# Latent attention scores: the rotary matmul over 128 partitions with half of them zero, in place of 64 partitions

## The reference, cut to what matters

```python
q = rms_norm(q, g_q); k = rms_norm(k, g_k)            # per head, 192 = 128 + 64 columns
q = concat([q[..., :128], rope(q[..., 128:], pos)])    # 64 rotary columns
k = concat([k[..., :128], rope(k[..., 128:], pos)])    # rotary key is shared by all heads before the norm
s = einsum('bqhe,bkhe->bhqk', qb, k) * 192 ** -0.5     # causal, then softmax, then @ v
```

## Time and profile before

| | |
|---|---|
| median of 3 runs | 1491.66 us (1490.26 to 1491.86) |
| span of the profiled execution | 1489.8 us |
| PE busy | 1456.9 us (98%) |
| PE weight loads busy | 1260.5 us (85%) |
| DVE, ACT, POOL busy | 43%, 46%, 48% |
| latent stage with its attention | about 76 to 342 us of the span |
| dilated stage | about 420 to 1400 us |

### The profile page before, as it was taken

One profiled execution on the slowest core, in us unless ns is written; L12 is line 12 of the kernel. 1 busy time (PEld: TensorE's weight loads), 2 busy tenths in 40 slices (PEclk: granted clock), 3 DMA queues, 4 the chain that ended last, 5 costly groups with the idle time before them and its releaser, 6 DMA issues.

```text
span 1489.8 us, 22557 instructions
## 1 busy us (share of the span) xinstructions
PE 1456.9 (98%) x8018; PEld 1260.5 (85%) x8018; DVE 635.0 (43%) x1024; ACT 686.8 (46%) x975; POOL 708.4 (48%) x332
## 2 busy tenths in 40 slices
PE   6999999999999999999999999999999999999998
PEld 4888888899988888888888888888887888888998
DVE  7455566544953234333334333433342333333332
ACT  4354555544334445444544544444544544444442
POOL 3443444433545444644553554564465355445432
PEclk9899999999999999999999999999999999999999
DMA  6443334335545554654554554555455455455444
GB/s 235 156 148 131 130 123 141 134 128 184 169 167 187 190 175 145 191 190 150 180 191 157 170 189 151 170 187 179 147 187 190 151 179 191 150 177 192 162 156 142
DMA packets 69344, 248.50 MB, mean 167 GB/s; under 512 B 7696, under 2 KB 8080, under 8 KB 69136
## 3 DMA queue, kind: packets, MB, share of 16 engines
q1 hardware_dynamic: 69120, 246.28, 48.7%
q10 hardware_dynamic: 144, 1.05, 0.2%
HBM read 245.20 MB, written 2.10 MB: 166 GB/s over the span
## 4 chain that ended last, share of the span: by engine, by line
PE 38%; issue 31%; POOL 26%; DVE 4%; POOLq 0%; DMA 0%; ACT 0%; SPq 0%; ACTq 0%; DVEq 0%
PE acc L1069 35%; POOL w_lo L378 21%; POOL root L392 2%; DVE xa_lo L712 1%; POOL phase L438 1%; POOL rms L389 1%; PE turn L1099 1%; PE pv_bank L1111 1%; PE score L1289 1%; DVE w_lo L698 1%; DVE prob L743 0%; DVE xb_hi L709 0%; POOL rms L396 0%; DVE xa_hi L709 0%; DVE res L980 0%
## 5 line engine op out<-in xcount | busy, mean ns | idle before, releaser
L378 POOL TENSOR_TENSOR w_lo<-raw,w_hi 128x1024 fp32r<-128x1024 f32 x232 | 574.1, 2475 | 636.5 <-ACT w_hi L462 636.3
L462 ACT ACTIVATE w_hi<-raw 128x1024 fp32r<-128x1024 f32 (+1 forms) x465 | 485.4, 1050 | 342.8 <-PE acc L1069 331.8
L698 DVE TENSOR_TENSOR w_lo<-raw,w_hi 128x1024 fp32r<-128x1024 f32 (+1 forms) x233 | 313.2, 1345 | 439.7 <-ACT w_hi L462 439.7
L1069 PE MATMUL acc<-w_hi,xa_hi 128*128 128x512 f32 (+1 forms) x1088 | 407.0, 374 | 10.7 <-DVE w_lo L698 10.7
L1069 PE MATMUL acc<-w_hi,xa_lo 128*128 128x512 f32 (+1 forms) x1088 | 399.0, 367 | 0.0
L1069 PE MATMUL acc<-w_lo,xa_hi 128*128 128x512 f32 (+1 forms) x1088 | 398.2, 366 | 0.0
L1069 PE MATMUL acc<-w_hi,xb_hi 128*128 128x512 f32 (+1 forms) x640 | 252.6, 395 | 4.3 <-POOL w_lo L378 2.4
L1069 PE MATMUL acc<-w_hi,xb_lo 128*128 128x512 f32 (+1 forms) x640 | 247.4, 387 | 0.0
L1069 PE MATMUL acc<-w_lo,xb_hi 128*128 128x512 f32 (+1 forms) x640 | 247.3, 386 | 0.0
L1069 PEld LDWEIGHTS acc<-w_hi,xa_hi 128*128 128x128 f32 x1088 | 206.6, 190 | 44.5 <-issue 13.4
L1069 PEld LDWEIGHTS acc<-w_hi,xa_lo 128*128 128x128 f32 x1088 | 206.2, 190 | 33.8
(11 more groups left out here) (116 smaller groups left out, 1076.1 us busy)
## 6 DMA issues: line engine op xcount, KB each, us to landing
raw<-in_w_b SPq DMA_DIRECT2D x320, 512.0 KB, 3.3
raw<-in_w_gate SPq DMA_DIRECT2D x32, 512.0 KB, 3.2
raw<-in_w_out_a SPq DMA_DIRECT2D x32, 512.0 KB, 3.3
raw<-in_w_out_b SPq DMA_DIRECT2D x32, 512.0 KB, 3.3
raw<-in_w_in SPq DMA_DIRECT2D x16, 512.0 KB, 4.3
raw<-in_w_kv SPq DMA_DIRECT2D x16, 512.0 KB, 3.3
raw<-in_w_q SPq DMA_DIRECT2D x16, 384.0 KB, 3.0
res<-in_xT SPq DMA_DIRECT2D x4, 512.0 KB, 7.3
```

The costliest lines, as they stand in the source:

```text
L378: nc.gpsimd.tensor_tensor(w[1][:, s, 0:width], raw[:, s, 0:width], w[0][:, s, 0:width].bitcast(F32), ALU.subtract).then_inc(lo_ready[1], 1)
L462: nc.scalar.activation(w[0][:, s, 0:width], raw[:, s, 0:width], ACT.Copy).then_inc(hi_ready, 1)
L698: nc.vector.tensor_tensor(w[1][:, s, 0:width], raw[:, s, 0:width], w[0][:, s, 0:width].bitcast(F32), ALU.subtract).then_inc(lo_ready[0], 1)
L1069: last = nc.tensor.matmul(out, x(a), y(b), start=start and k == 0, stop=stop and k == 2, **more)
```

## The change

Two buffers `q_ropes` of 128 x 512, in parts of `qT` and `v` that only the dilated stage uses, are set to zero at the start by POOL. In place of one copy of the block of both heads, ACT copies head 0's 64 partitions into columns 0 to 255 and head 1's into columns 256 to 511; the other 64 partitions of each half stay zero. The second matmul of a score then takes all 128 partitions of `q_ropes` and of the rotary block of `kT`. Keys are handled as before. Line numbers in the changed file are 1 to 14 lower for the same statement.

```diff
+SET_UPS = 3 + 2
...
+        q_ropes = (qT[:, 2 * 512:3 * 512], v[:, 2 * 512:3 * 512])
...
-            pool.wait_ge(set_up, 3)
+            for q_rope in q_ropes:
+                nc.gpsimd.memset(q_rope, 0.0).then_inc(set_up, 1)
+            pool.wait_ge(set_up, SET_UPS)
...
-            def mla_turned(dst, par, rnd, g, rope_bank):
+            def mla_keys_turned(par, rnd):
...
+            def mla_queries_turned(par, rnd):
+
+                act.wait_ge(turn_full, rnd + 1)
+                nc.scalar.activation(qT[:, par * 512:(par + 1) * 512], turn[:], ACT.Copy, scale=gn("q_nope"))
+                for h in range(2):
+                    a, b = h * ROPE, (h + 1) * ROPE
+                    last = nc.scalar.activation(q_ropes[par][a:b, h * SEQ:(h + 1) * SEQ], pv_bank[a:b, P:P + SEQ],
+                                                ACT.Copy)
+                last.then_inc(turn_read, 1)
...
-            pe.wait_ge(set_up, 3)
+            pe.wait_ge(set_up, SET_UPS)
...
             def mla_score(U, par, u):
...
-                nc.tensor.matmul(score[:, 0:n], qT[:, base + h * SEQ + t * P:base + h * SEQ + (t + 1) * P],
-                                 kT[:, base + h * SEQ:base + h * SEQ + n], start=True, stop=False)
-                a, b = h * ROPE, (h + 1) * ROPE
-                nc.tensor.matmul(score[:, 0:n], qT[a:b, base + 512 + t * P:base + 512 + (t + 1) * P],
-                                 kT[a:b, base + 512:base + 512 + n], start=False, stop=True).then_inc(scored, 1)
+                at = h * SEQ + t * P
+                nc.tensor.matmul(score[:, 0:n], qT[:, par * 512 + at:par * 512 + at + P],
+                                 kT[:, k_0 + h * SEQ:k_0 + h * SEQ + n], start=True, stop=False)
+                nc.tensor.matmul(score[:, 0:n], q_ropes[par][:, at:at + P], kT[:, k_0 + 512:k_0 + 512 + n],
+                                 start=False, stop=True).then_inc(scored, 1)
```

More of the change, by code:

```diff
@@ L564, in mla_keys @@
                                      acc[:, pair, :, 2 * P:4 * P], ACT.Copy).then_inc(v_act, 1)
-            def mla_turned(dst, par, rnd, g, rope_bank):
+            def mla_keys_turned(par, rnd):
                 base = par * 768
                 act.wait_ge(turn_full, rnd + 1)
-                nc.scalar.activation(dst[:, base:base + 512], turn[:], ACT.Copy, scale=g)
-                nc.scalar.activation(dst[:, base + 512:base + 768], rope_bank[:, P:P + SEQ], ACT.Copy)\
+                nc.scalar.activation(kT[:, base:base + 512], turn[:], ACT.Copy, scale=gn("k_nope"))
+                nc.scalar.activation(kT[:, base + 512:base + 768], og_bank[:, P:P + SEQ], ACT.Copy)\
                     .then_inc(turn_read, 1)
+            def mla_queries_turned(par, rnd):
[6 more added lines that the diff above has]
+                last.then_inc(turn_read, 1)
             def mla_attend(i, s, later):
@@ L590, in mla_pair @@
                     if s == 2 and later:
-                        mla_turned(qT, 1 - par, mla_round(i, 0), gn("q_nope"), pv_bank)
+                        mla_queries_turned(1 - par, mla_round(i, 0))
                     if s == 3:
-                        mla_turned(kT, par, mla_round(i, 1) if later else 4, gn("k_nope"), og_bank)
+                        mla_keys_turned(par, mla_round(i, 1) if later else 4)
                     mla_attend(i, s, later)
@@ L606, in _ @@
                 if k == 2:
-                    mla_turned(qT, 1, mla_round(PAIRS, 0), gn("q_nope"), pv_bank)
+                    mla_queries_turned(1, mla_round(PAIRS, 0))
                 mla_attend(PAIRS, k, 2)
@@ L1174, in mla_score @@
             def mla_score(U, par, u):
+                k_0 = par * 768
                 h, t = u // 2, u % 2
-                base = par * 768
                 if u:
```

## The result

The changed kernel takes **1479.39 us** (median of 4 runs, 1477.86 to 1480.95) against 1490.96 us for the kernel before in the same measurement (4 runs, 1489.89 to 1491.86): a ratio of 0.9926, 95% interval 0.9912 to 0.9940. The medians are 11.6 us apart; by the ratio the kernel is 0.74% faster, 11.0 us. The forecast was 1480.5 us, 0.75% faster, own range 1479 to 1483: it held. The profiled execution has a span of 1476.1 us, against 1489.8 before and 1478.6 forecast; it is the fastest of the four.

The account below looks back on a forecast made before the run. PE bounds the latent stage, but savings count only where no wait stands behind them. Six pairs save 8.8 us, the first 0.9, the last 1.5: 11.2 in all, giving 1480.5 us, range 1479 to 1483.

Parts of the forecast that it names:

- The cost of 64 rows: Around each unit's 64-row score matmul PE loses 0.20 us on entry and 0.18 on exit; 128 rows save 0.38.
- unit 0: A pair's score unit before the key turn; saves 0.35 us, its exit going into transposes with shorter loads.
- The rival that the gaps belong to the accumulation: Units keep their time and only the race counts: 1488.5 to 1493.2 us; chance 0.08.
- The race: Before the key turn, the second copy delays POOL's `w_lo`; DVE's rotary write starts first by 0.02 us, removing PE's 0.53 wait.
- the price taken from the earlier trace: ACT's second copy delays `w_hi` by 0.26 us, or 0.28 from a copy over 64 partitions.
- The key turn with unit 0: Step 3: the 0.53 us wait goes and unit 0's 0.35 counts, 0.88 in each of six pairs.
- The swallowed part: PE's saving of 0.58 us a pair, unit 2's exit and unit 3's both ends, is lost waiting for `og`.
- the wait for `og`: Step 1, seven times: PE's wait grows to about 1.2 us, part of it showing in step 0 at the gate.
- The sum: 1.46 us a pair, 8.8 in six pairs; 0.9 in the first pair, 1.5 in the last; 11.2 in all.
- The fills: POOL's two zero fills at the start cost at most 1.2 us each, hidden in its 9.9 us wait for `w_hi`.
- that standstill: PE's stop of some 2 us before 99, then clock 0.81; compared with about 1.8 before 898, clock 1.00.

Follow-up runs that it names:

- e1: Kernel before, with the second score matmul over all 128 rows of the old block and ACT's one copy kept; 1484.37 us, ratio 0.9960.
- e3: Kernel before, with the two matmuls of a score in the other order, 64 rows first; 1489.75 us (1 run).
- e10: Kernel before, with ACT's copy of the turned rotary queries cut into four: two column halves for each 64 partitions; 1487.97 us (1 run).
- e11: Kernel before, with ACT's copy of the turned rotary queries cut into two column halves over all 128 partitions; 1491.44 us (1 run).
- e9: Changed kernel, with three unused sums of 128 columns on DVE ahead of its rotary write; 1487.78 us, ratio 0.9984 to the kernel before.
- e4: Changed kernel, with ACT in step 5 computing `w_hi` before the gate's tanh; 1472.86 us, ratio 0.9884 to the kernel before.
- e5: Kernel before, with ACT in step 5 computing `w_hi` before the gate's tanh; 1487.12 us, ratio 0.9979.
- e8: Changed kernel with e4's order in later pairs; in the first pair DVE computes the gate in step 5, before its `w_lo`; 1473.23 us, ratio 0.9885.
- e6: Kernel before, with one more ACT copy of a single column between L570 and L571 for the queries; 1490.62 us, ratio 1.0005.

## Why the prediction was right

**The cost of 64 rows: right, size too.** Forecast 0.38 a unit, and 0.35 for unit 0. Units 1 to 3 save 0.39, 0.39 and 0.40, whether they have 128 or 256 keys, and unit 0 saves 0.34 where no wait stands behind it. e1 shows that the rows alone do it, e3 that it goes where the rows change. The rival that the gaps belong to the accumulation is out. What the Trainium skill says in TensorEngine Tiling (Array Packing), Key Properties, of a drain at a change of the tiling mode agrees with e3; some 0.2 us on either side is this case's number for it.

**The race: right in its outcome, its margin mis-sized.** The forecast had `w_hi` 0.26 later, with 0.5 as the bound if ACT had to finish a copy first, and DVE ahead by 0.02. It was the bound: 0.77 instead of 0.26 from the first copy, 0.51 later, and DVE 0.28 ahead. The term that was mis-sized is the price taken from the earlier trace rows: that row's successor starts 0.28 behind a copy of 64 partitions because both begin at partition 0. The copy of head 1 begins at 64, and the earlier trace rows has no such change; e10 and e11 show that this is what counts. The time is the same as forecast since a race won by 0.02 or by 0.28 is won alike; the write at 110 us, 0.02 ahead, shows that the small margin would have done too. The key turn with unit 0 gave 0.87 a pair for a forecast 0.88. What the Trainium skill says of DVE and GpSimd in SBUF — State Buffer, Who interferes with whom, agrees with e9: the first to issue holds the port throughout, and the other one waits (the write takes 1.78 to 1.79 us in place of 0.42). It does so down to a small difference only: with POOL 0.01 ahead by its recorded start, DVE still went first.

**The swallowed part: right in size, wrong in place.** 0.58 a pair was to be lost; 0.55 was lost at the gate and 0.04 behind it. But I expected the wait for `og` to grow to 1.2 us and only a part to show at the gate. It is the other way round: PE's timeline has both,

```profile
213.00 0.49 PE L1067 MATMUL acc<-w_hi,xb_hi 128*128 128x512 f32 x1 [0.25 <-DVE gate L808]
...
219.75 0.33 PE L1117 MATMUL og_bank<-ident,og 128*128 128x128 f32 x1 [0.41 <-DVE og L798]
```

and 0.41 is no more than the 0.38 of the earlier trace rows. The gate comes first in PE's order, takes nearly all of what PE had saved, and PE then comes to `og` almost as late as ever. The idle time in such a row counts from a modelled end, so 0.25 stands for 0.55 by the starts. That both waits hang on ACT's late work in step 5 is what e4 and e5 show: moved forward, it frees the gate wholly in e4, takes the wait for `og` from 2.6 us to 1.3, and removes it in e5.

**The sum.** Forecast 1.46 a pair, measured 1.46, and no term of the pair is off by more than 0.02, so the sum owes nothing to errors that cancel. In all 11.2 forecast, 11.3 in the trace and 11.6 in the medians. That the trace's other 2.4 us are missing from the forecast is not its fault: they come and go between profiles. The fills cost nothing, as said. None of the waits from 130 to 340 us made the clock fall; its window reads 1.00.

```profile
130.00:340.00 210.00, 206.00 (x1480) 194.43 (x1479) 113.01 (x329) 113.46 (x236) 91.22 (x43) 1.00 0.45 141
```

What stays open is why the clock falls behind the standstill before 99 in six of nine profiles and not in the others. The prediction set that standstill beside one of about 1.8 us before 898, which is the distance of two starts; counted as the 1.93 is, that one has 1.39 us:

```profile
897.86 0.49 PE L1069 MATMUL acc<-w_hi,xb_hi 128*128 128x512 f32 x1 [1.39 <-POOL w_lo L378]
```

## What to carry to other kernels

A matmul over fewer rows between full ones can cost more than zeros in the unused rows: look for a load that starts together with its matmul instead of ahead of it, and price both sides of the change. A gain on the bound engine is worth what the next wait on its path leaves of it, so the same edit may be worth 2.8 or 6.3 us; find the chain behind that wait and move its first link forward. Where two engines contend for memory, more work on a third can be a gain, and such a gain is fragile: know the margin, because 0.6 us on an engine that is idle more than half of the time took back three quarters of it here. Know it in every pass of the loop, too: here it was 0.28 us in six pairs and 0.02 in another.

## What the runs showed of the hardware

ACT overlaps an instruction with the one before it (a copy of 256 columns takes 0.37 us and the next starts after 0.26) as long as the start partition stays; from 0 to 64 and from 64 to 0 it finished the first, at 0.11 to 0.14 us for each change behind copies of 256 columns and about the same behind 128 (e10).

In the contest of DVE and POOL, a DVE write that started 0.01 us behind POOL still went first; one that started 0.12 behind (e8), 0.19 (e6), 0.24, 0.31 (e9) or 0.49 (e5) was held until POOL was through, and ended 0.28 behind it each time. Where between 0.01 and 0.12 it turns was not measured.
